# The gated recurrence's factor chain interleaved with the last eight projection blocks

## The chip, the cores and the metric

The kernel runs on one core of a Trainium2 chip. The metric is the device time of one execution in microseconds (us). It has five engines with their own instruction queues: TensorE (PE, with its weight loads shown as PEld), VectorE (DVE), ScalarE (ACT), GpSimd (POOL) and SyncE (SP, which here only issues DMAs). Each queue is worked off in order, and engines wait for each other through semaphores. All times on the axis "us" are counted from the start of the profiled span.

## What is computed

The reference is one transformer block followed by a second one. The part that matters here is the token mixing of the first block: the input of 512 tokens, normed, is multiplied with a wide matrix, and 16 blocks of 128 columns of the product feed a gated linear recurrence with 4 heads of 128. Its four inputs are q, f, i and og (4 blocks each).

```python
q = silu(q_raw); f = lb + (1 - lb) * sigmoid(f_raw); k = 1 - f; v = i_raw
b = cumsum(log(f))                        # within chunks of 64 tokens
ref = b at token 31 of the chunk; b_last = b at token 63
scores = (q * exp(b - ref)) @ (k * exp(ref - b)).T, causal, within a chunk
kv_n = (k * exp(b_last - b)).T @ v        # one state update for each chunk
state = exp(b_last) * state + kv_n        # over the 8 chunks
out = scores @ v + (q * exp(b)) @ state_before
y = rmsnorm(out) * sigmoid(og)
```

The "factor chain" is the elementwise part: sigmoid, the affine map to f and k, log, the running sum over 64 tokens, two shifted copies of it, four exponentials and four products. Beside it stand 24 "gate" blocks, further projections whose results are biased and stored to device memory for later; 8 of them lie in this stage.

## The kernel before

Everything is fp32. A projection block is 8 steps (one for each 128 rows of the weights) of three matmuls of 128x512 (lines 615 to 617: high weights by high operand, high weights by low operand, low weights by high operand), so 24 matmuls into one of the PSUM banks 0 to 3, taken in turn. The weights of a block are one "unit" of 128x1024: SP loads it (L453), ACT makes its high part (`split`, L1214, called by `units`), POOL its low part (`low`, L539). There are four slots for units, and ACT's `units(1)` beside block m splits the unit of block m+3, which it may do once PE has finished block m-1. `blocks(k)` on ACT is k such splits. Behind each unit's load SP also issues one 512 KB copy of a table that is needed much later (L462).

A bank is given back when DVE has copied it out (`copy_blocks`, L1890, semaphore `block_free`, counted in order); PE waits for that in `claim` before it writes the bank again. In the stage at hand (PE lines 888 to 941), blocks 0 to 3 are q (tile `hg_q`), 4 to 7 f (`hg_f`), 8 to 11 i (`hg_i`), 12 to 15 og (`hg_og`). Then PE turns the four heads of i (`turn`, L719: four 128x128 transposes of a head into bank 4 or 7, which ACT copies out by `turned`, L1334, before the bank is used again), runs six gate blocks (banks 0 and 1 in turn; ACT adds the bias and copies out, L1238, semaphore `gate_ready`, and issues the store, L1242), waits for `hg_factors_ready`, turns the four heads of K2, does the 32 score products (L911), and then alternates seven state products (L922) with quarters of the two remaining gate blocks.

ACT (lines 1540 to 1566) does all nine remaining splits first, then waits until all 16 blocks are copied out, then Silu of q, Sigmoid of f, Sigmoid of og, the four `turned` of V, the log, five gate copies (`gate1`), and when DVE has signalled `hg_shift`, the exponentials Q1, K1, Q2, DEC and, behind the second shift, K2; then the sixth gate copy and the four `turned` of K2. A change of function set costs ACT a table load, shown as ACT_TABLE_LOAD.

DVE (lines 2150 to 2183) copies out blocks 7 to 15 first and then runs its part of the chain: four affine maps (L2157), k (L2159), six scan steps of a copy and an addition each (L2166, L2167), two shifts (L2173), four products (L2179 to L2183). The second shift waits for two exponentials, because it overwrites their input.

Of the kernel before, what the change touches and what calls it, by code (L numbers as in the profile page):

```python
# [11 lines left out]
ACT = mybir.ActivationFunctionType  # L12
AX_X = mybir.AxisListType.X

P = 128
TOK = 512
TT = TOK // P
# [186 lines left out]
def program(nc, a):  # L204

    with ExitStack() as ctx:
# [380 lines left out]
        def _(pe):  # L587
# [45 lines left out]
            def x_ops():  # L633
                return (lambda k: XH[:, k, :]), (lambda k: XL[:, k, :])
# [4 lines left out]
            def operand(total):  # L639

                n["operand"] = n.get("operand", 0) + total
                pe.wait_ge(sem("operand_ready"), n["operand"])
# [249 lines left out]
            operand(DC)  # L892
            for m in range(8, 16):
                block_(DC, *x_ops())


            pe.wait_ge(sem("block_free"), n["freed"])
            for h in range(HEADS):
                turn([ZI[:, h, t * P:(t + 1) * P] for t in range(TT)])
# [298 lines left out]
        def _(act):  # L1198
# [341 lines left out]
            blocks(9)  # L1540

            act.wait_ge(sem("block_free"), n["freed"])
            act.activation(ZQ[:], ZQ[:], ACT.Silu).then_inc(sem("hg_q_ready"), 1)
            act.activation(ZF[:], ZF[:], ACT.Sigmoid).then_inc(sem("hg_sigmoid"), 1)
            act.activation(ZOG[:], ZOG[:], ACT.Sigmoid).then_inc(sem("hg_og_ready"), 1)
            for h in range(HEADS):
                turned(VT[:, h, :])
            act.dma_start(TRI[:], a["tri"]).then_inc(sem("tri_loaded"), 16)
            act.wait_ge(sem("hg_f_ready"), 1)
            act.activation(B0[:], ZF[:], ACT.Ln).then_inc(sem("hg_log"), 1)  # L1550
            for _ in range(5):
                gate1()
# [9 lines left out]
            gate1()  # L1562
            for h in range(HEADS):
                turned(K2T[:, h, :])
# [302 lines left out]
        def _(dve):  # L1867
# [284 lines left out]
            for z in (ZI, ZOG):  # L2152
                copy_blocks(z, 4)
            st.skip(8, 0)
# [4 lines left out]
            dve.tensor_scalar(KF[:], ZF[:], -1.0, 1.0, ALU.mult, ALU.add).then_inc(sem("hg_f_ready"), 1)  # L2159
            dve.wait_ge(sem("hg_log"), 1)  # L2160
# [3 lines left out]
            for i in range(6):  # L2164
                src, dst = chunks[i % 2], chunks[1 - i % 2]
                link(dve.tensor_copy(dst[:, :, 0:d], src[:, :, 0:d]))  # L2166
                link(dve.tensor_tensor(dst[:, :, d:CH], src[:, :, d:CH], src[:, :, 0:CH - d], ALU.add))  # L2167
                d *= 2

# [5 lines left out]
            shifted(CH // 2 - 1, 1)  # L2175
            dve.wait_ge(sem("hg_exp"), 2)
            shifted(CH - 1, -1)
            dve.wait_ge(sem("hg_q_ready"), 1)
# [689 lines left out]
```

## Time and profile before

| quantity | value |
|---|---|
| median of 3 runs | 3729.67 us |
| lowest, highest run | 3727.66, 3734.19 us |
| profiled execution: device time | 3727.16 us |
| profiled execution: span of the trace | 3725.3 us |
| busy share of the span: PE, PEld, DVE, ACT, POOL | 95%, 80%, 56%, 37%, 49% |
| mean granted TensorE clock | 0.976 of full speed |

The device time is 1.86 us longer than the span, which runs from the first to the last instruction. The profile's clock column is the share of TensorE's full clock (2.4 GHz) that was granted: 1.00 is 2.4 GHz and 0.50 is 1.2 GHz. The stage of the recurrence lies at 487 to 698 us of 3725. A share of PE's busy time over the whole span hides what happens in so short a stage, so the stage has to be read from its own waits and stretches. "x8" behind a row means that instructions of one kind that follow each other directly are merged, and the duration is that of all. The bracket at the end of a row of the timeline is the engine's idle time just before and who ended it.

### The profile page before, as it was taken

Reading aid. Unit: us, or ns where it says so; the run is one execution under the profiler, and the core shown is the slowest. Engines: PE = TensorE matmul, PEld = TensorE weight load, DVE = VectorE, ACT = ScalarE, POOL = GpSimd, SP = SyncE. Lnnn points to the kernel's source line nnn. Section 1 sums busy time; section 2 is a strip of 40 time slices with the busy share of each in tenths; the row PEclk is TensorE's granted clock in tenths of the full one; section 3 lists DMA queues with packets and bytes.
Section 4 is the critical chain, followed back from the end, with each engine's and each line's share of the span. In section 5 each row is a group of like instructions: output and inputs, shape, how many; then the busy total and the mean of one; then the engine's idle time right before and its main releaser. Section 6 shows DMA issues by size and latency. Waiting matters only on the chain. (4 is left out here: it accounts for less than half of the span.)

```text
span 3725.3 us, 49795 instructions
## 1 busy us (share of the span) xinstructions
PE 3532.4 (95%) x17547; PEld 2996.4 (80%) x17547; DVE 2092.5 (56%) x4197; ACT 1386.8 (37%) x1941; POOL 1838.5 (49%) x909
## 2 busy tenths in 40 slices
PE   8999997999999999997988999989999999999999
PEld 5777766777787688773676766779999999999999
DVE  4653055222234344125666255459999997677776
ACT  4333234233244322222323345323345454444443
POOL 5676433233243344341333301435566676788886
PEclk9999998999999999997999999999999999999999
DMA  6997544444567299331424312685559999899996
GB/s 241 386 381 247 159 150 140 127 149 149 158 206 246 72 297 290 113 100 42 137 80 134 101 54 71 220 325 176 164 164 317 344 352 342 325 388 391 383 383 234
DMA packets 458130, 813.81 MB, mean 218 GB/s; under 512 B 31544, under 2 KB 308984, under 8 KB 455322
## 3 DMA queue, kind: packets, MB, share of 16 engines
q1 hardware_dynamic: 278416, 436.07, 35.5%
q10 hardware_dynamic: 142666, 241.11, 18.3%
q0 software_dynamic: 36864, 134.23, 9.5%
q8 instruction: 108, 1.77, 0.2%
q14 instruction: 76, 0.62, 0.1%
HBM read 682.84 MB, written 195.56 MB: 236 GB/s over the span
## 5 line engine op out<-in xcount | busy, mean ns | idle before, releaser
L539 POOL TENSOR_TENSOR weights_lo<-weights_raw,weights_hi 128x1024 fp32r<-128x1024 f32 x649 | 1592.7, 2459 | 1816.1 <-ACT weights_hi L1214 1692.7
L615 PE MATMUL bank<-operand_hi,weights_hi 128*128 128x512 f32 (+1 forms) x2856 | 1093.4, 383 | 54.3 <-DVE operand_lo L1916 18.7
L617 PE MATMUL bank<-operand_hi,weights_lo 128*128 128x512 f32 (+1 forms) x2856 | 1064.5, 373 | 0.0
L616 PE MATMUL bank<-operand_lo,weights_hi 128*128 128x512 f32 (+1 forms) x2856 | 1063.4, 372 | 0.0
L1214 ACT ACTIVATE weights_hi<-weights_raw 128x1024 fp32r<-128x1024 f32 x649 | 683.3, 1056 | 858.6 <-PE bank L617 559.4
L615 PEld LDWEIGHTS bank<-operand_hi,weights_hi 128*128 128x128 f32 x2856 | 541.3, 190 | 145.9 <-DVE operand_lo L1916 25.1
L616 PEld LDWEIGHTS bank<-operand_lo,weights_hi 128*128 128x128 f32 x2856 | 542.1, 190 | 74.4 <-issue 5.5
L617 PEld LDWEIGHTS bank<-operand_hi,weights_lo 128*128 128x128 f32 x2856 | 540.2, 189 | 74.7
L615 PE MATMUL bank<-expert_hi,weights_hi 128*128 128x384 f32 x1024 | 345.1, 337 | 0.0
L617 PE MATMUL bank<-expert_hi,weights_lo 128*128 128x384 f32 x1024 | 345.0, 337 | 0.0
L616 PE MATMUL bank<-expert_lo,weights_hi 128*128 128x384 f32 x1024 | 345.0, 337 | 0.0
L615 PEld LDWEIGHTS bank<-expert_hi,weights_hi 128*128 128x128 f32 x1024 | 192.3, 188 | 0.0
L617 PEld LDWEIGHTS bank<-expert_hi,weights_lo 128*128 128x128 f32 x1024 | 192.3, 188 | 0.0
L616 PEld LDWEIGHTS bank<-expert_lo,weights_hi 128*128 128x128 f32 x1024 | 192.3, 188 | 0.0
L2632 DVE SCALAR_TENSOR_TENSOR bank<-gathered_experts,slot_weight,bank 128x512 f32<-128x512 f32 x254 | 178.8, 749 | 16.5 <-DMA gathered_experts<-expert_table_v,expert_index 14.6
L1773 ACT ACTIVATE gate_stage<-bank 128x512 f32<-128x512 f32 x96 | 104.2, 1086 | 175.3 <-PE bank L1133 162.5
L1960 DVE STREAM_TRANSPOSE expert_turned<-expert_rows 128x1024 f32<-128x1024 f32 x90 | 111.7, 1242 | 101.4 <-DMA expert_table_u<-expert_turned 79.8
L2541 DVE CUSTOM_DVE_ANT_0 gathered_experts<-gathered_experts,bank 128x512 f32<-128x512 f32 x256 | 161.9, 679 | 5.5 <-DMA gathered_experts<-expert_table_u,expert_index 5.4
L1821 ACT ACTIVATE expert_hi<-bank 128x384 fp32r<-128x384 f32 x128 | 63.0, 492 | 270.9 <-DVE bank L2580 264.7
L2557 DVE TENSOR_SCALAR one_hot_i<-iota,expert_ijg_t 128x128 f32<-128x128 f32 x384 | 160.1, 417 | 1.2 <-ACT expert_ijg_t L1334 1.2
L615 PE MATMUL bank<-hidden_hi,weights_hi 128*128 128x512 f32 x352 | 144.4, 410 | 2.0 <-DVE hidden_lo L2002 2.0
L617 PE MATMUL bank<-hidden_hi,weights_lo 128*128 128x512 f32 x352 | 139.5, 396 | 0.0
(397 smaller groups left out, 4899.5 us busy)
## 6 DMA issues: line engine op xcount, KB each, us to landing
weights_raw<-in_w_ffn_gu SPq DMA_DIRECT2D x132, 512.0 KB
expert_table_v<-in_w_peer_out SPq DMA_DIRECT2D x120, 512.0 KB, 5.5
weights_raw<-in_w_peer_ahead SPq DMA_DIRECT2D x120, 512.0 KB
weights_raw<-in_w_peer_out SPq DMA_DIRECT2D x120, 512.0 KB
expert_table_u<-expert_turned ACTq DMA_DIRECT2D x360, 128.0 KB, 4.7
expert_rows<-in_w_peer_ahead ACTq DMA_DIRECT2D x82, 512.0 KB, 6.7
peer_gates<-gate_stage SPq DMA_DIRECT2D x24, 1024.0 KB
expert_gates<-peer_gates ACTq DMA_DIRECT2D x16, 1536.0 KB
```

Of the source, the lines that this page charges most:

```text
L539: pool.tensor_tensor(LO[:, slot, :], RAW[:, slot, :], HI[:, slot, :].bitcast(F32), ALU.subtract).then_inc(sem("lo_ready"), 1)
L615: pe.matmul(out, wh, hi(k), start=(k == 0), stop=False)
L616: pe.matmul(out, wh, lo(k), start=False, stop=False)
L617: ins = pe.matmul(out, wl, hi(k), start=False, stop=(k == kc - 1))
L1214: act.activation(HI[:, slot, :], RAW[:, slot, :], ACT.Copy).then_inc(sem("hi_ready"), 1)
L1773: act.activation(STG[:, s, :, 4 * (q % 4):4 * (q % 4) + 4].rearrange("p j t -> p t j"), BANK[5 + q % 2][:].rearrange("p (t j) -> p t j", t ...
L1821: act.activation(dst, src, ACT.Copy).then_inc(sem("expert_high"), 1)
L1960: return dve.transpose(dst[:].rearrange("p (b c y) -> p c b y", b=4, c=DC), src[:].rearrange("p (c b y) -> p c b y", b=4, c=DC))
L2541: ins = dve.tensor_tensor_reduce(half, half, tokens_in[h][:], 1.0, 0.0, ALU.mult, ALU.add, DOT[:, s, h:h + 1])
L2557: dve.tensor_scalar(OI[:, u, :], IOTA[:], IJGT[:, 0, token], None, ALU.is_equal)
L2632: ins = dve.scalar_tensor_tensor(sums_of[h][:], half, AW[:, s:s + 1], sums_of[h][:], ALU.mult, ALU.add)
```

## The change

PE turns heads 0 and 1 of i behind block 13 and heads 2 and 3 behind block 14, having waited only for the copies of blocks 8 to 11, and no longer waits for all 16 blocks. ACT works the sigmoid of f, the log, the Silu of q and the copies of V in between its splits, does the exponentials right behind, and moves the sigmoid of og and five of the gate copies behind them. DVE starts its chain behind block 7 and puts the copies of blocks 8 to 15 in between the steps of the chain. No arithmetic is added or taken away; the products, the kv part and what follows are as they were.

```diff
--- before.py
+++ after.py
@@ -890,13 +890,15 @@
             for m in range(3, 8):
                 block_(DC, *rest)
             operand(DC)
+            inputs = n["freed"] + 4
             for m in range(8, 16):
                 block_(DC, *x_ops())
-
-
-            pe.wait_ge(sem("block_free"), n["freed"])
-            for h in range(HEADS):
-                turn([ZI[:, h, t * P:(t + 1) * P] for t in range(TT)])
+                if m == 13:
+                    pe.wait_ge(sem("block_free"), inputs)
+                for h in {13: (0, 1), 14: (2, 3)}.get(m, ()):
+                    turn([ZI[:, h, t * P:(t + 1) * P] for t in range(TT)])
+
+
             for _ in range(6):
                 gate_block()
             pe.wait_ge(sem("hg_factors_ready"), 1)
@@ -1537,19 +1539,22 @@
             highs(XH, XFM, 3, None, 3)
             blocks(1)
             highs(XH, XFM, 2, None, 6)
-            blocks(9)
-
-            act.wait_ge(sem("block_free"), n["freed"])
-            act.activation(ZQ[:], ZQ[:], ACT.Silu).then_inc(sem("hg_q_ready"), 1)
+            blocks(2)
+            act.wait_ge(sem("block_free"), n["freed"] - 1)
             act.activation(ZF[:], ZF[:], ACT.Sigmoid).then_inc(sem("hg_sigmoid"), 1)
-            act.activation(ZOG[:], ZOG[:], ACT.Sigmoid).then_inc(sem("hg_og_ready"), 1)
-            for h in range(HEADS):
-                turned(VT[:, h, :])
-            act.dma_start(TRI[:], a["tri"]).then_inc(sem("tri_loaded"), 16)
+            blocks(1)
             act.wait_ge(sem("hg_f_ready"), 1)
             act.activation(B0[:], ZF[:], ACT.Ln).then_inc(sem("hg_log"), 1)
-            for _ in range(5):
-                gate1()
+            blocks(1)
+            act.activation(ZQ[:], ZQ[:], ACT.Silu).then_inc(sem("hg_q_ready"), 1)
+            blocks(3)
+            for h in range(2):
+                turned(VT[:, h, :])
+            blocks(1)
+            for h in range(2, HEADS):
+                turned(VT[:, h, :])
+            blocks(1)
+            act.dma_start(TRI[:], a["tri"]).then_inc(sem("tri_loaded"), 16)
 
             act.wait_ge(sem("hg_shift"), 1)
             act.activation(Q1[:], B1[:], ACT.Exp).then_inc(sem("hg_exp"), 1)
@@ -1560,6 +1565,10 @@
             act.wait_ge(sem("hg_shift"), 2)
             act.activation(K2[:], B1[:], ACT.Exp).then_inc(sem("hg_exp"), 1)
             gate1()
+            act.wait_ge(sem("block_free"), n["freed"])
+            act.activation(ZOG[:], ZOG[:], ACT.Sigmoid).then_inc(sem("hg_og_ready"), 1)
+            for _ in range(5):
+                gate1()
             for h in range(HEADS):
                 turned(K2T[:, h, :])
             for _ in range(2):
@@ -2149,14 +2158,12 @@
 
             normed(XFM, HT, XH, XL, TOK, lambda c: vec("mix_pre", c), beside=first_blocks)
             copy_blocks(ZF, 3, first=1, scaled=True)
-            for z in (ZI, ZOG):
-                copy_blocks(z, 4)
-            st.skip(8, 0)
             dve.wait_ge(sem("hg_sigmoid"), 1)
             for h in range(HEADS):
                 link(dve.tensor_scalar(ZF[:, h, :], ZF[:, h, :], LB[:, 5, h:h + 1], LB[:, 2, h:h + 1],
                                        ALU.mult, ALU.add))
             dve.tensor_scalar(KF[:], ZF[:], -1.0, 1.0, ALU.mult, ALU.add).then_inc(sem("hg_f_ready"), 1)
+            copy_blocks(ZI, 1)
             dve.wait_ge(sem("hg_log"), 1)
 
             chunks = [b[:].rearrange("p h (n c) -> p (h n) c", c=CH) for b in (B0, B1)]
@@ -2166,6 +2173,10 @@
                 link(dve.tensor_copy(dst[:, :, 0:d], src[:, :, 0:d]))
                 link(dve.tensor_tensor(dst[:, :, d:CH], src[:, :, d:CH], src[:, :, 0:CH - d], ALU.add))
                 d *= 2
+                if i in (0, 1, 3):
+                    copy_blocks(ZI, 1, first=(1, 2, 2, 3)[i])
+                elif i >= 4:
+                    copy_blocks(ZOG, 1, first=i - 4)
 
             def shifted(at, sign):
                 edge = chunks[0][:, :, at:at + 1].to_broadcast([P, HEADS * NCH, CH])
@@ -2173,8 +2184,11 @@
                 dve.tensor_tensor(chunks[1], *pair, ALU.subtract).then_inc(sem("hg_shift"), 1)
 
             shifted(CH // 2 - 1, 1)
+            copy_blocks(ZOG, 1, first=2)
             dve.wait_ge(sem("hg_exp"), 2)
             shifted(CH - 1, -1)
+            copy_blocks(ZOG, 1, first=3)
+            st.skip(8, 0)
             dve.wait_ge(sem("hg_q_ready"), 1)
             link(dve.tensor_tensor(Q1[:], Q1[:], ZQ[:], ALU.mult))
             link(dve.tensor_tensor(K1[:], K1[:], KF[:], ALU.mult))
```

## Rows read from the trace of the kernel before

**Rows 1.** The page, busy time and share of each engine.

```profile
PE 3532.4 (95%) x17547; PEld 2996.4 (80%) x17547; DVE 2092.5 (56%) x4197; ACT 1386.8 (37%) x1941; POOL 1838.5 (49%) x909
```

**Rows 2.** Busy time by stretch of the stage; the first line names the columns.

```profile
core 0: us, PE busy (x) PEld busy (x) DVE busy (x) ACT busy (x) POOL busy (x), PEclk, DMA share, GB/s
530.90:574.40 43.50, 43.50 (x193) 35.84 (x191) 5.54 (x8) 9.78 (x9) 19.12 (x8) 1.00 0.63 193
574.40:618.70 44.30, 37.16 (x161) 30.46 (x160) 30.47 (x19) 25.17 (x23) 16.36 (x5) 0.92 0.56 172
618.70:639.60 20.90, 6.58 (x82) 5.80 (x81) 15.86 (x8) 9.47 (x11) 4.72 (x2) 0.59 0.21 68
```

**Rows 3.** The two longest PE waits, 570 to 680 us: total, times, longest.

```profile
PE bank L719 <- DVE hg_k L2183: 14.3, 1, 14.3
PE bank L719 <- ACT hg_v L1334: 6.4, 1, 6.4
```

**Rows 4.** PE's timeline: start, duration, line, tiles, idle before.

```profile
575.36 1.09 PE L719 MATMUL bank<-identity,hg_i 128*128 128x128 f32 x8 [0.79 <-DVE hg_og L1896]
582.81 1.97 PE L719 MATMUL bank<-identity,hg_i 128*128 128x128 f32 x8 [6.36 <-ACT hg_v L1334]
584.43 0.78 PE L615 MATMUL bank<-operand_hi,weights_hi 128*128 128x512 f32 x1
...
587.73 0.39 PE L617 MATMUL bank<-operand_hi,weights_lo 128*128 128x512 f32 x1
...
633.04 3.77 PE L719 MATMUL bank<-identity,hg_k 128*128 128x128 f32 x16 [14.32 <-DVE hg_k L2183]
636.74 2.92 PE L911 MATMUL bank<-hg_q,hg_k 128*64 128x64 f32 x64
```

**Rows 5.** The clock in one stretch of the second i turn.

```profile
582.20:584.90 2.70, 2.09 (x9) 2.09 (x10) 1.79 (x3) 1.72 (x5) 0.00 (x0) 0.50 0.03 6
```

**Rows 6.** DVE's timeline of the stage.

```profile
536.53 0.69 DVE L1896 COPY hg_i<-bank 128x512 f32<-128x512 f32 x1 [4.75 <-PE bank L617]
...
574.61 0.69 DVE L1896 COPY hg_og<-bank 128x512 f32<-128x512 f32 x1 [4.75 <-PE bank L617]
580.51 2.29 DVE L2157 TENSOR_SCALAR hg_f<-hg_f,lower_bound 128x512 f32<-128x512 f32 x4 [5.20 <-ACT hg_f L1544]
582.83 1.23 DVE L2159 TENSOR_SCALAR hg_k<-hg_f 128x2048 f32<-128x2048 f32 x1
...
588.91 2.26 DVE L2167 TENSOR_TENSOR hg_b<-hg_b 128x2016 f32<-128x2016 f32 x1
591.21 2.28 DVE L2166 COPY hg_b<-hg_b 128x64 f32<-128x64 f32 x1
...
602.73 2.02 DVE L2167 TENSOR_TENSOR hg_b<-hg_b 128x1792 f32<-128x1792 f32 x1
...
611.10 4.36 DVE L2173 TENSOR_TENSOR hg_b<-hg_b 128x2048 f32<-128x2048 f32 x1
...
630.69 2.29 DVE L2183 TENSOR_TENSOR hg_k<-hg_k,hg_k 128x2048 f32<-128x2048 f32 x1
```

**Rows 7.** POOL's timeline: a low part alone and one that met DVE.

```profile
537.82 2.39 POOL L539 TENSOR_TENSOR weights_lo<-weights_raw,weights_hi 128x1024 fp32r<-128x1024 f32 x1 [3.04 <-ACT weights_hi L1214]
...
589.75 3.67 POOL L539 TENSOR_TENSOR weights_lo<-weights_raw,weights_hi 128x1024 fp32r<-128x1024 f32 x1 [16.90 <-ACT weights_hi L1214]
```

**Rows 8.** ACT's timeline of the stage.

```profile
531.15 1.06 ACT L1214 ACTIVATE weights_hi<-weights_raw 128x1024 fp32r<-128x1024 f32 x1 [4.56 <-PE bank L617]
...
577.27 1.28 ACT L1544 ACT_TABLE_LOAD   x1
578.56 1.91 ACT L1544 ACTIVATE hg_f<-hg_f 128x2048 f32<-128x2048 f32 x1
...
582.18 1.07 ACT L1334 ACTIVATE hg_v<-bank 128x512 f32<-128x512 f32 x2
...
591.62 0.69 ACT L1238 ACTIVATE squares<-bank,vectors 128x512 f32<-128x512 f32 x1 [2.03 <-PE bank L617]
```

## Prediction

> **What bounds the kernel now.** The page comes first: PE is busy for 95% of the span, and beside its own weight loads (80%) no engine for more than 56% [rows 1], so only time in which PE stands still, or runs at a low clock, can be won. Whether there is any in the stage that changes is seen in its stretches [rows 2]. From 530.9 to 574.4 us, blocks 8 to 15, PE is busy for all of 43.5 us, and DVE for 5.5 and ACT for 9.8: both idle beside a full PE. From 574.4 to 618.7 PE lacks 7.1 us, and from 618.7 to 639.6 it works 6.6 of 20.9. Its waits name the causes [rows 3]: 14.3 us on the last product of the factor chain (L2183) and 6.4 us on the first copy of V (L1334), which ACT reaches only behind three activations of 128x2048; 0.79 us, the bracket of the first turn, go to the last copy of og [rows 4]. So the chain, not PE, sets when the K2 turns begin. The DMA share in these stretches is 0.63, 0.56 and 0.21 [rows 2], so transfers do not set the end of them.
>
> **What the change takes away.** First the waits: 14.32 + 6.36 + 0.79 = 21.5 us [rows 4], if each is covered (below).
>
> Then the clock. Behind both long waits PE ran at the lower level: in the second pair of i turns the granted clock was 0.50, which is 1.2 GHz [rows 5], after 6.4 us of standing; the stretch of the K2 turns has a mean of 0.59 [rows 2]. What that cost is read from rows at either level. The second pair of i turns took 1.97 us where the first took 1.09 [rows 4]: 0.9 us. In the first gate block, 584.43 to 587.73 are eight starts of matmuls in 3.30 us [rows 4]. At full clock a block of 24 takes 5.44 us (copies at 536.53 and 574.61 are seven blocks apart [rows 6]: 38.08 / 7), eight starts 1.8 us: 1.5 us. The K2 turns took from 633.04 to 636.74, 3.7 us [rows 4]. At full clock PE needs 4 x 0.45 (eight transposes that started within 0.9, from the 1.09 less the tail of the last), but two banks wait for ACT's copies of some 0.6 us each [rows 8] and for the last gate copy before them; I take 3.0: 0.7 us. The 64 small matmuls of the scores took 2.9 us [rows 4]. Full clock gives between 1.45 (half) and 2.9; I take 1.9, nearer to the half because the turns halved: 1.0 us. Sum of the clock: 4.1 us, bounds 2.4 (no gain on scores and K2 turns) to 5.3.
>
> **What it adds.** PE gets one wait at block 13, satisfied by then, and two more changes between blocks and turns. No row shows such a change without a wait; the bound from above is the 0.79 us that the first turn waited, from below 0; I take 0.2. The 16 i transposes are moved, not added. ACT gets a fifth table load, 1.28 us [rows 8], because the sigmoid of og now stands behind the exponentials; it lies beside gate blocks.
>
> **Is the work really covered?** I lay the changed queues out by durations of the rows. Block m ends at 536.5 + 5.44 (m - 8).
> - ACT: the split of block 8 ends at 532.2 [rows 8]; table load 1.28 and Sigmoid 1.9 give f at 535.4.
> - DVE: four maps 2.3, k 1.23 (a fixed-scalar form at the rate of the maps, 2048 elements in one instruction, so at most their 2.3; I take 1.2) give f at 539.0; block 8 is copied out by 539.7. ACT does the log by 541.0 behind the split of block 9 at 537.7.
> - DVE's scan. In the kernel before, steps 0 to 3 ended at 604.75 and all six at 611.1, with the first addition at 588.91 [rows 6], so some 16 and 22.3 us, and one low part of POOL for each 5.4 us already lay beside them. That is the rate it will meet again. With the copies of blocks between them, 0.73 each, block 11 is given back by 541.0 + 16 + 2.2 = 559.3 and the first shift ends at 541.0 + 22.3 + 3.7 + 2.3 = 569.3, at worst two more us as the 4.36 shows [rows 6].
> - PE wants block 11's copy at 563.7, behind block 13: 4.4 us to spare. Turns 0.9, block 14 until 570.1, turns 0.9, block 15 until 576.4.
> - ACT copies V of heads 2 and 3 by 571.8 (1.07 for two [rows 8]), splits until 572.9, issues one DMA 0.35, table load 1.3: 574.5. The shift is ready. Q1, K1, Q2 at 1.8 each and DEC end at 580.3. DVE shifts again from 578.2, ends 580.5. K2 by 582.4, split of the fourth gate block's unit by 583.4, copy of gate 0 (0.69 [rows 8]) by 584.1.
> - PE: gate 0 from 576.4, gate 1 until 587.3. Gate 2 wants the bank of gate 0: 3.2 us to spare. ACT then loads a table, 1.3, does the Sigmoid of og, 1.9, a split, 1.1, and copies gate 1 by 589.4; gate 3 wants it at 592.7: 3.3 us. From then on the ring is as before.
> - DVE behind its second shift: one copy 0.7, four products 9.2, and one collision with a low part of 2.1: factors at 592.9. PE ends the sixth gate block at 576.4 + 32.6 = 609.0. The wait of 14.3 is gone with 16 us to spare.
>
> SP's loads and table copies follow POOL's low parts, and their number is the same; the next loads are three units ahead of PE, 16 us, so an ACT or POOL that is some us late does not reach PE. If one of the covers goes, its excess comes back to PE one for one.
>
> The next thing after the K2 turns, 0.2 us of issue and the scores, is the state part, whose pace PE and DVE share as before. **Sum:** 21.5 + 4.1 - 0.2 = 25.4 us. The profiled execution took 3727.16 (span 3725.3 plus 1.86 around it): 3701.8. It lies 2.5 below the median 3729.67, so the median is forecast at 3704.3.
>
> One rule of the Trainium skill bears on the covers. A low part alone took 2.39 us, and one that met an addition of DVE 3.67; the scan copy of 128x64 that began at 591.21 ended at 593.49, when the low part that began at 589.75 ended (593.42) [rows 6, 7]. "SBUF — State Buffer", section "SBUF: two separate sides", calls the port pair of VectorE and GpSimd an exclusive lock, held for the whole instruction by whichever came first, for DVE instructions with two SBUF inputs or in a two-port mode. By this rule the rows agree; it is what rival 3 is made of.
>
> **Rivals.**
> 1. Late copies of the gate banks. ACT now does everything in one line from 564 to 590, with only 3.2 us to spare twice. If that line is 3 to 12 us later than laid out (a copy of V that waits for PE, a shift that meets low parts), PE stands up to 9 us before gate 2 and the clock may fall. For it: the smallest slack of all. Against it: its terms are rows. Gain 16 to 25, middle 20: 3709.
> 2. PE's gain is given back later, or the change does not do what it says. The stage from 3000 us on could be paced by something that doesn't move with PE. A rule that would give this: the same page, section "A bandwidth-pool intuition that's wrong", calls HBM almost always the bottleneck end to end. Here the DMA share was 0.21 to 0.63 in the stage [rows 2], and loads are issued behind POOL's and PE's progress, so they move with PE. No gain would mean 3730, half of it 3717.
> 3. Slower: DVE's steps and POOL's low parts exclude each other, and now PE waits for what lies between the steps. The place is the line of 18 instructions up to the first shift (4 maps, k, 12 of the scan, the shift), behind it ACT's exponentials and so the gate banks. By rows a collision costs DVE up to 2.07 (4.36 against 2.29 [rows 6]). The line has 5.2 us to spare at the shift and 3.2 at the gates, 8.4 together. PE loses all of the 25.4 when it is 34 us late, 1.9 us for each of the 18 beyond what the scan's rows hold already. At the full 2.4 of a low part each, 43 us, the time is 25.4 - (43 - 8.4) = 9 us slower, 3739. Against it: POOL does one low part for each block, five or six in this line, not eighteen. It decides only if each low part hits three instructions, which an exclusive lock alone can't do.
>
> **How the numbers follow.** Forecast 0.74 (3699 to 3709), rival 1 0.13 (3705 to 3716), rival 2 0.10, of which 0.03 halfway at 3717 and 0.07 within 4 us of 3730, rival 3 0.03. The bounds of the unknown costs are 25.4 - 2.3 and + 1.4; the runs before scatter from 2 below to 4.5 above their median. So 3698 to 3716 holds some 0.86, and a little more than asked for is left in since one piece of slack is thin. About 0.2%, 7.5 us, is what a measurement of this kernel can tell from no change. Faster by more: 0.74 + 0.13 + 0.03 = 0.90; within: 0.07; slower: 0.03.
>
> **What the profile after would show.** Right: PE's three waits on L719 are gone, PE is busy throughout from 530 to about 610, the granted clock stays 1.00 there, the K2 turns begin near 609 and the state products near 614 instead of 639.6, and DVE's last product lies some 16 us ahead of the K2 turns. Rival 1: a wait of PE L615 on ACT's copy L1238 at 587 or 593. Rival 2: the state products 25 us earlier, but the span not, with a longer wait later. Rival 3: PE waits on DVE's copies (L1896) at 564, or on ACT behind DVE, and DVE rows of 4 us. Wrong would be the whole sum if the waits moved to PE's claims of banks, or if the stage were 25 us shorter and another part longer.

## The result, and the profile after

| | before | changed |
|---|---|---|
| median of 4 runs, measured together | 3728.66 us | 3703.52 us |
| lowest, highest | 3726.43, 3734.19 | 3697.55, 3707.28 |
| ratio, 95% interval | | 0.993, 0.9913 to 0.9946 |
| span of the profiled execution | 3725.3 us | 3698.8 us |
| mean granted clock | 0.976 | 0.978 |

The changed kernel is 25.1 us faster by these medians, where 25.4 were forecast (3704.3, measured 3703.5); the interval of the ratio allows 20.1 to 32.4 us. Measured a second time, against 15 runs of the kernel before, it was 30.3 us faster (r0 below). The interval of that ratio allows 24.6 to 34.7 us, so the two agree.

The stage by stretches, after (columns as in the first line; the clock is the eighth value, before the DMA share):

```profile
core 0: us, PE busy (x) PEld busy (x) DVE busy (x) ACT busy (x) POOL busy (x), PEclk, DMA share, GB/s
530.10:576.40 46.30, 46.30 (x214) 38.46 (x213) 31.05 (x26) 24.62 (x21) 23.01 (x8) 1.00 0.60 186
576.40:608.10 31.70, 31.70 (x141) 26.21 (x140) 17.91 (x7) 16.85 (x17) 19.48 (x6) 1.00 0.75 233
608.10:613.20 5.10, 4.14 (x82) 3.59 (x80) 0.69 (x2) 3.81 (x6) 0.21 (x1) 1.00 0.92 270
```

Against [rows 2]: PE is busy in all of 46.3 and of 31.7 us, DVE now works 31.1 us and ACT 24.6 beside the last eight blocks instead of 5.5 and 9.8, and the granted clock is 1.00 throughout, where it had been 0.92 and 0.59 from the end of the blocks on. POOL is busy for 42.7 us in the three stretches, and was for 40.2 in those of [rows 2].

PE's waits from 530 to 680 us, after (total, times, longest):

```profile
PE bank L615 <- DVE dil_qkv L1905: 6.2, 1, 6.2
PE bank L719 <- ACT hg_k2t L1336: 1.0, 1, 1.0
```

All three waits of [rows 3, 4] are gone. The wait for K2's copy is the one that the prediction put inside its 3.0 us for the K2 turns; the one of 6.2 us lies behind the stage and was there before the change too.

PE's timeline, after (start, duration, line, tiles):

```profile
562.78 1.03 PE L719 MATMUL bank<-identity,hg_i 128*128 128x128 f32 x8
...
569.13 1.03 PE L719 MATMUL bank<-identity,hg_i 128*128 128x128 f32 x8
...
608.11 1.03 PE L719 MATMUL bank<-identity,hg_k 128*128 128x128 f32 x8
610.10 1.14 PE L719 MATMUL bank<-identity,hg_k 128*128 128x128 f32 x8 [0.95 <-ACT hg_k2t L1336]
611.18 2.08 PE L913 MATMUL bank<-hg_q,hg_k 128*64 128x64 f32 x64
613.19 1.04 PE L924 MATMUL bank<-hg_v,hg_k2t 64*128 64x128 f32 x7
```

The second pair of i turns takes 1.03 us and not 1.97, the K2 turns 3.07 (611.18 - 608.11) and not 3.70, the scores 2.01 (613.19 - 611.18) and not 2.85 [rows 4]. Since other parts of the trace move by some us from one profile to the next, the experiments are read by one length: from the first matmul of block 8 to the first state product (L922 before, L924 after). It was 639.59 - 530.89 = 108.70 us and is 613.19 - 530.14 = 83.05: **25.65 us less**. From the state product to the end of the span it was 3085.7 us and is 3085.6. The other 0.75 us of the span lie ahead of the stage. That the two rests agree to 0.1 us is chance: over the profiles of all kernels here in which nothing behind the stage is altered, this rest lies between 3079.8 (e9) and 3085.7 us (before). In none of them is it longer than in the kernel before, so nothing that the trace shows was given back later.

The length after is accounted for: 14 blocks of 5.44 (8 projection and 6 gate blocks) are 76.2, two pairs of i turns 0.91 each (569.13 - 562.78 less a block), K2 turns 3.07, scores 2.01: 83.1 us. There is no room for a cost of changing between blocks and turns.

DVE's timeline, after, at the steps that the prediction used:

```profile
534.72 2.29 DVE L2163 TENSOR_SCALAR hg_f<-hg_f,lower_bound 128x512 f32<-128x512 f32 x4 [3.69 <-ACT hg_f L1544]
...
543.55 1.69 DVE L2173 COPY hg_b<-hg_b 128x64 f32<-128x64 f32 x1
545.28 2.23 DVE L2174 TENSOR_TENSOR hg_b<-hg_b 128x1984 f32<-128x1984 f32 x1
...
555.04 0.69 DVE L1905 COPY hg_i<-bank 128x512 f32<-128x512 f32 x1
...
564.05 2.28 DVE L2184 TENSOR_TENSOR hg_b<-hg_b 128x2048 f32<-128x2048 f32 x1
...
576.86 2.29 DVE L2184 TENSOR_TENSOR hg_b<-hg_b 128x2048 f32<-128x2048 f32 x1 [6.84 <-ACT hg_k L1561]
...
584.31 4.38 DVE L2196 TENSOR_TENSOR hg_q<-hg_q,hg_q 128x2048 f32<-128x2048 f32 x1
588.73 4.38 DVE L2197 TENSOR_TENSOR hg_k<-hg_k,hg_k 128x2048 f32<-128x2048 f32 x1
```

And ACT's:

```profile
563.41 1.09 ACT L1336 ACTIVATE hg_v<-bank 128x512 f32<-128x512 f32 x2 [4.76 <-PE bank L719]
...
573.11 1.92 ACT L1560 ACTIVATE hg_q<-hg_b 128x2048 f32<-128x2048 f32 x1
...
581.96 0.67 ACT L1240 ACTIVATE squares<-bank,vectors 128x512 f32<-128x512 f32 x1
...
587.10 0.66 ACT L1240 ACTIVATE squares<-bank,vectors 128x512 f32<-128x512 f32 x1
```

Block 11 is copied out by 555.7, the first shift ends at 566.3, and ACT comes to it only at 573.1. The copy of gate 0 ends at 582.6; gate 2 begins at 586.35 (608.11 less four blocks): 3.7 us to spare. The copy of gate 1 ends at 587.8, gate 3 begins at 591.8: 4.0. The factors are ready at 593.1, 15.0 us ahead of the K2 turns.

### The profile page after: what moved, and what is told of

It reads as the page before. It is cut to its first block and busy times, and to the rows that moved or that the text cites. A ratio compares the mean times of both kernels' runs of the same rounds, so it can differ in the third digit from the quotient of the medians.

```text
span 3698.8 us, 49801 instructions
## 1 busy us (share of the span) xinstructions
PE 3528.6 (95%) x17547; PEld 2993.7 (81%) x17547; DVE 2091.1 (57%) x4197; ACT 1387.2 (38%) x1942; POOL 1842.2 (50%) x909
## 5 line engine op out<-in xcount | busy, mean ns | idle before, releaser
L615 PEld LDWEIGHTS bank<-operand_hi,weights_hi 128*128 128x128 f32 x2856 | 541.4, 190 | 145.2 <-DVE operand_lo L1925 24.6
L2646 DVE SCALAR_TENSOR_TENSOR bank<-gathered_experts,slot_weight,bank 128x512 f32<-128x512 f32 x254 | 178.8, 750 | 20.8 <-DMA gathered_experts<-expert_table_v,expert_index 18.9
L2572 DVE TENSOR_SCALAR one_hot_j<-iota,expert_ijg_t 128x128 f32<-128x128 f32 x384 | 142.7, 372 | 0.0
```

Of the source, the lines that this page charges most:

```text
L615: pe.matmul(out, wh, hi(k), start=(k == 0), stop=False)
L2572: return dve.tensor_scalar(OJ[:, u, :], IOTA[:], IJGT[:, 1, token], IJGT[:, 2, token], ALU.is_equal, ALU.mult)
L2646: ins = dve.scalar_tensor_tensor(sums_of[h][:], half, AW[:, s:s + 1], sums_of[h][:], ALU.mult, ALU.add)
```

## Experiments

Lengths are those from block 8 to the first state product; the changed kernel has 83.05. The last column has the device time and that of the kernel before measured with it; where a kernel ran once only, no conclusion is drawn from its time, as the profiles reach block 8 anywhere between 528.9 and 538.2 us and the rest behind the stage varies by 6 us.

| kernel | length, us | against changed | time; before, us (runs) |
|---|---|---|---|
| before | 108.70 | +25.65 | |
| changed; again (r0) | 83.05; 83.06 | | r0 3701.16; 3731.45 (5; 15) |
| e1 before, early i turns alone | 107.80 | +24.75 | 3726.32; 3731.45 (10; 15) |
| e2 changed, i turns late | 84.52 | +1.47 | 3705.97; 3728.24 (1; 1) |
| e10 changed, block copies behind the scan | 92.35 | +9.30 | 3709.69; 3728.24 (1; 1) |
| e3 changed, 2 more exponentials | 83.50 | +0.45 | 3703.13; 3731.31 (1; 1) |
| e4 changed, 5 more exponentials | 91.70 | +8.65 | 3709.31; 3731.31 (1; 1) |
| e5 changed, 4 more products | 86.07 | +3.02 | 3701.77; 3731.31 (1; 1) |
| e6 changed, 9 more products | 98.27 | +15.22 | 3721.92; 3731.31 (1; 1) |
| e9 before, PE kept busy | 106.70 | +23.65 | 3724.38; 3728.24 (1; 1) |
| e7 changed, sums before the dilated blocks | 83.06 | +0.01 | 3697.29; 3728.24 (1; 1) |
| e8 as e7, and K2 turns around gate 5 | 81.86 | -1.19 | 3693.99; 3731.45 (5; 15) |
| e11 as e8, split behind the norm's exponential | 81.86 | -1.19 | 3698.11; 3730.56 (4; 7) |

### Repeat, and where the time is

r0 is the changed kernel unaltered.

> The changed kernel unaltered, beside the kernel before and the next two on the same chip. My theory (the stage alone is shorter: 21.5 us of waits and about 4 us of low clock gone, all else moved forward as a whole): 25.6 us under the kernel before, ratio 0.9931; the first state product about 26 us earlier. Rival (part of the gain is given back in a later stage): the stage 25 us shorter but the time less than 20 us.

Measured: 3701.16 us against 3731.45, ratio 0.992 (0.9907 to 0.9934). The length is 83.06, and the rest behind it 3083.2 us, not longer than the 3085.7 of the kernel before. The stage alone is shorter, as the first theory has it.

### Which part of the change carries the gain

e1 takes only the turns:

```diff
             for m in range(8, 16):
                 block_(DC, *x_ops())
+                if m == 13:
+                    pe.wait_ge(sem("block_free"), inputs)
+                for h in {13: (0, 1), 14: (2, 3)}.get(m, ()):
+                    turn([ZI[:, h, t * P:(t + 1) * P] for t in range(TT)])
```

with ACT's four `turned` of V between its last splits. DVE's order is that of the kernel before.

> The kernel before with one part of the change: PE turns i behind blocks 13 and 14 and ACT copies V there; the factor chain stays where it was, behind block 15. Theory (one chain, from the last block copied out to the factors, sets when the K2 turns begin, so a wait of PE before it is worth nothing by itself): PE's waits of 0.8 and 6.4 us go, but its wait for the factors grows from 14.3 to about 20; the chain begins 1 us earlier because ACT has no V copies in front of the log; also a new wait of some 2.7 us before the third gate block. Gain 1 us. Rival (the waits add up, each is worth its length, as the prediction's sum has it): gain 0.8 + 6.4 + 2.4 of clock = 9.5 us.

e1's waits of PE in the stage:

```profile
PE bank L719 <- DVE hg_k L2189: 18.9, 1, 18.9
PE bank L615 <- ACT squares L1240: 2.2, 1, 2.2
```

The waits of 0.8 and 6.4 us are gone, and the wait for the factors has grown from 14.3 to 18.9. The length falls by 0.90 us, where lengths that add up would have given 9.5. The turns in front of it make the last block come 1.8 us later, and the chain from that block's copy to the factors takes 55.6 instead of 58.4 us, since V is copied by then. The runs went from 3731.45 to 3726.32 us (ratio 0.9985, 0.9975 to 0.9995), a gain of 1.9 to 9.3 us by the interval. That leaves out the 9.5 narrowly and the 0.9 too; the length in the trace is of one execution each, and where the runs' other microseconds come from stays open. A wait in front of another wait on the same chain was worth next to nothing: PE only arrives earlier at the later one.

e2 is the other half, the early chain without the early turns (PE still asks only for blocks 8 to 11 before it turns i):

```diff
-                if m == 13:
+                if m == 15:
                     pe.wait_ge(sem("block_free"), inputs)
-                for h in {13: (0, 1), 14: (2, 3)}.get(m, ()):
+                for h in {15: (0, 1, 2, 3)}.get(m, ()):
```

> The changed kernel with the four i turns back behind block 15 and ACT's copies of V behind its last split; the chain stays early. Theory: PE waits about 0.4 us for the two banks, and ACT's exponentials start 5 us later (578.3 instead of 573.1), which is more than the 3.7 us that the first gate copy had to spare, so PE waits 1.3 to 1.8 us before the third gate block: the first state product 2 us later than in the changed kernel. Rival (the early turns carry their full 7 us of waits and 2.4 of clock): 9 us later.

```profile
PE bank L719 <- ACT hg_k2t L1336: 1.0, 1, 1.0
PE bank L615 <- ACT squares L1240: 0.7, 1, 0.7
PE bank L719 <- ACT hg_v L1336: 0.3, 1, 0.3
```

These waits of PE (beside the 6.2 behind the stage) are 0.7 us before the third gate block and 0.3 between the turns. The length grows by 1.47 us, where 2 were expected. So 24.2 of the 25.65 us come with the early chain alone, 0.9 with the early turns alone. The early turns are worth little in either order, 0.9 us without the early chain and 1.5 with it; the early chain is worth nearly everything in either. It also takes away the waits at the turns of i: with the turns in their old place only 0.3 us of the old 7.2 is left there, since ACT no longer has Silu and two Sigmoids to do in front of V.

### Why the copies stand between the scan steps

e10:

```diff
-                if i in (0, 1, 3):
-                    copy_blocks(ZI, 1, first=(1, 2, 2, 3)[i])
-                elif i >= 4:
-                    copy_blocks(ZOG, 1, first=i - 4)
+                if i == 5:
+                    copy_blocks(ZI, 3, first=1)
+                    copy_blocks(ZOG, 2)
```

> The changed kernel with DVE's copies of blocks 9 to 13 behind all six scan steps and not between them. Theory: the scan ends near 560.5, block 13 cannot have the bank of block 9 before 561.2 and not at 557.3 as in the changed kernel: PE waits 3.8 us there, and the first state product comes 3.8 us later, with no further wait (the clock stays full, ACT moves with PE). Rival (the copies beside the scan cost DVE's chain more than they save PE): no wait of PE on a copy, and the first state product no later.

DVE's timeline of e10, and the block of PE that waited:

```profile
541.57 0.35 DVE L2173 COPY hg_b<-hg_b 128x32 f32<-128x32 f32 x1 [1.39 <-ACT hg_b L1547]
...
544.24 2.30 DVE L2173 COPY hg_b<-hg_b 128x64 f32<-128x64 f32 x1
...
560.81 3.25 DVE L2174 TENSOR_TENSOR hg_b<-hg_b 128x1024 f32<-128x1024 f32 x1
564.09 1.89 DVE L1905 COPY hg_i<-bank 128x512 f32<-128x512 f32 x3
```

```profile
564.93 0.76 PE L615 MATMUL bank<-operand_hi,weights_hi 128*128 128x512 f32 x1 [6.13 <-DVE hg_i L1905]
```

The mechanism is as expected, the size is not: 9.3 us against 3.8. The scan was expected to end at 560.5 us on the changed kernel's axis, and ended at 562.8 on it (564.1 less 1.3, by which e10's block 8 starts later), so the wait was 2.3 us longer than expected. It took 22.5 us (541.57 to 564.06) without any copy in between; in the changed kernel it took 23.2 (540.26 to 563.41) with four copies of 0.69 in between. The four copies, 2.8 us by themselves, cost 0.7. POOL's rows of the changed kernel show why:

```profile
542.50 2.68 POOL L539 TENSOR_TENSOR weights_lo<-weights_raw,weights_hi 128x1024 fp32r<-128x1024 f32 x1 [1.94 <-ACT weights_hi L1216]
547.95 2.40 POOL L539 TENSOR_TENSOR weights_lo<-weights_raw,weights_hi 128x1024 fp32r<-128x1024 f32 x1 [2.77 <-ACT weights_hi L1216]
553.38 3.89 POOL L539 TENSOR_TENSOR weights_lo<-weights_raw,weights_hi 128x1024 fp32r<-128x1024 f32 x1 [3.04 <-ACT weights_hi L1216]
```

The copy of block 11 (555.04 to 555.73) ran while POOL's low part of 553.38 to 557.27 was under way, and took its 0.69 us. It reads PSUM. The additions and copies of the scan have their inputs in SBUF and do not run beside a low part: the copy of 128x64 at 543.55 takes 1.69 us and ends at 545.24, 0.06 us after the low part of 542.50. Put between them, the PSUM copies used time in which the chain would have stood anyway. Behind the wait of 6.1 us the clock was at 0.50 until 571 us, which is the other 3.2 of the 9.3.

### How late ACT may be

e3 and e4 put two and five more exponentials in front of the first one:

```diff
             act.wait_ge(sem("hg_shift"), 1)
+            for i in range(5):
+                act.activation(Q1[:], B1[:], ACT.Exp).then_inc(sem("padded"), 1)
+                act.wait_ge(sem("padded"), i + 1)
             act.activation(Q1[:], B1[:], ACT.Exp).then_inc(sem("hg_exp"), 1)
```

> The changed kernel with two more exponentials of 128x2048 on ACT before the first one, 3.8 us with their waits: it makes the line of ACT late on purpose. Theory (the gate banks have 3.7 us to spare, more comes back one for one): PE waits 0 to 0.5 us before the third gate block, the first state product at most 0.5 us later. Rival (the slack is not real, a later ACT is felt at once): 3.8 us later.

> The changed kernel with five more exponentials on ACT before the first one, 9.5 us. Theory: PE waits 5.8 us before the third gate block and nowhere else in the stage, and the clock may fall for a few us behind it; the first state product 5.8 to 7 us later. Rival (the ring of two banks passes the lateness on to the next gate blocks): 9 us or more.

In e3 PE waited 0.15 us, and the length is 0.45 us greater; the other 0.3 us stay unexplained. e4, PE's row at the third gate block, and the clock of four stretches around it (eighth value):

```profile
593.49 0.77 PE L615 MATMUL bank<-operand_hi,weights_hi 128*128 128x512 f32 x1 [5.99 <-ACT squares L1240]
```

```profile
589.00:591.00 2.00, 0.00 (x0) 0.00 (x0) 2.00 (x3) 1.59 (x3) 0.00 (x0) 1.00 0.00 0
591.00:593.00 2.00, 0.00 (x0) 0.00 (x0) 1.97 (x2) 2.00 (x3) 0.07 (x1) 0.69 0.01 4
593.50:598.00 4.50, 4.50 (x11) 3.57 (x12) 4.47 (x2) 4.24 (x4) 3.75 (x1) 0.50 0.16 58
599.00:602.00 3.00, 3.00 (x15) 2.47 (x14) 2.96 (x2) 1.33 (x2) 3.00 (x2) 1.00 0.96 311
```

The spare time is real: 3.8 us of lateness cost 0.45, and of 9.5 us PE waited 6.0. Beyond it the price is more than one for one. The wait is the one expected (5.8), the price is above the expected 5.8 to 7: the clock fell while PE stood and stayed at 1.2 GHz for some 5 us behind the wait, 8.65 - 5.99 = 2.7 us more. The wait occurred once, so the ring did not pass it on, and the rival falls.

### How late DVE may be

e5 and e6 put four and nine more products of 128x2048 in front of DVE's first:

```diff
+            for _ in range(4):
+                link(dve.tensor_tensor(SC[:].rearrange("p h t c -> p (h t c)"),
+                                       ZQ[:].rearrange("p h t -> p (h t)"),
+                                       KF[:].rearrange("p h t -> p (h t)"), ALU.mult))
             link(dve.tensor_tensor(Q1[:], Q1[:], ZQ[:], ALU.mult))
```

> The changed kernel with four more products of 128x2048 on DVE before its first product, at least 9.2 us; with their collisions with POOL's low parts up to 17. Theory (factors have 15.0 us to spare, from 593.1 to PE's K2 turns at 608.1): the factors at 602.4 to 608, no wait of PE for them, the first state product within 0.5 us of the changed kernel's. Rival (the lock starves POOL and PE waits for a low part of the weights): a wait of PE on L539 and 2 us or more.

> The changed kernel with nine more products on DVE, at least 20.7 us. Theory: factors at 614 to 620, so PE waits 6 to 12 us for them, the granted clock falls in that wait if it is long enough (it fell in the kernel before within waits of 6.4 and 14.3 us), and the K2 turns and scores take 1 to 1.6 us more: the first state product 6 to 14 us later. Rival (POOL's low parts come late as well): a wait of PE on L539 before the factors are late.

DVE's products in e5, then PE's K2 turns in e5 and in e6:

```profile
583.16 13.43 DVE L2194 TENSOR_TENSOR hg_scores<-hg_q,hg_k 128x2048 f32<-128x2048 f32 x4
596.63 4.38 DVE L2195 TENSOR_TENSOR hg_q<-hg_q,hg_q 128x2048 f32<-128x2048 f32 x1
...
609.85 4.36 DVE L2199 TENSOR_TENSOR hg_k<-hg_k,hg_k 128x2048 f32<-128x2048 f32 x1
```

```profile
614.26 3.49 PE L719 MATMUL bank<-identity,hg_k 128*128 128x128 f32 x16 [2.50 <-DVE hg_k L2199]
```

```profile
630.47 3.77 PE L719 MATMUL bank<-identity,hg_k 128*128 128x128 f32 x16 [14.16 <-DVE hg_k L2199]
```

Eight products took from 583.2 to 614.2, 31.0 us instead of 8 x 2.3 = 18.4. POOL did six low parts in that time, so each cost DVE 2.1 us. The factors of e5, expected at 602 to 608 on the changed kernel's axis, came at 610.7 there (614.2 less 3.5, by which its block 8 starts later), and PE waited 2.5 us. There was no wait of PE on a low part, so the rival falls: what comes late is DVE. The theory of e5 fails too, since it had no wait at all and at most 0.5 us. The clock had fallen within those 2.5 us; e5's clock just before the turns and in their first 3 us (eighth value):

```profile
613.00:614.00 1.00, 0.00 (x0) 0.00 (x0) 1.00 (x1) 0.00 (x0) 0.00 (x0) 0.96 0.88 147
614.00:617.00 3.00, 2.73 (x13) 2.36 (x14) 1.97 (x2) 1.20 (x2) 0.00 (x0) 0.50 1.00 332
```

Eight of the turns took 1.97 us, as at the lower level in [rows 4]. In e6 the wait is 14.2 us, above the 6 to 12 expected, and the turns take the 3.77 us that they took in the kernel before; the length grows by 15.2, above the 14 of the range. In e5 the 9.2 us of added work made DVE 17.6 us late at the factors (610.7 against 593.1). By that ratio the 15.0 us of spare time hold some 8 us of such work; this is an estimate, no run has that much.

### The clock by itself

e9 is the kernel before with matmuls of no use while PE would stand (they write a bank that is not in use):

```diff
             for h in range(HEADS):
                 turn([ZI[:, h, t * P:(t + 1) * P] for t in range(TT)])
+                if h == 1:
+                    idle_work(26)
             for _ in range(6):
                 gate_block()
+            idle_work(58)
             pe.wait_ge(sem("hg_factors_ready"), 1)
```

> The kernel before with 26 matmuls of no use between the second and third i turn and 58 before its wait for the factors, so that PE never stands still for long there; the wait itself stays with the chain. It tells the clock's share from the wait's. Theory (the clock costs what the rows at the two levels say): the granted clock stays 1.00 through the stage, K2 turns near 3.0 us instead of 3.7 and scores 2.0 instead of 2.9, the first gate block 5.4 and not 6.9; from the factors' end (633.0 in the kernel before) to the first state product 5.1 us instead of 6.6, so about 1.6 us gained, and up to 1 more if V is copied sooner. Rival (the clock's 4.1 us come back whatever the wait does): 4 us gained.

```profile
637.37 3.51 PE L719 MATMUL bank<-identity,hg_k 128*128 128x128 f32 x16 [2.36 <-DVE hg_k L2190]
```

The length falls by 2.0 us, where 1.6 to 2.6 were expected. DVE's chain was 0.9 us shorter (from its last block copy to the factors 57.5 instead of 58.4 us), since V was copied sooner; the rest, 1.1, is from the factors to the first state product, 5.5 us instead of 6.6. It is less than the 1.5 expected, because the useless work ended 2.4 us too soon and the granted clock was 0.50 again from 637.4 to 640 us, in most of the turns. So the clock behind the last wait of the chain cost about what the rows say. The first gate block ran at full clock now, and of the 2.0 us none is left for it: the clock behind an earlier wait cost nothing, because the later wait absorbed it. The rival (4 us whatever the wait does) falls. When PE's waits went in the changed kernel, though, no later wait was left to absorb anything, and there all of it counted.

### A version that is faster than both

The largest wait left near the stage is the 6.2 us on the first dilated block. e7 moves the sums of each head's norm by one block, e8 also turns heads 0 and 1 of K2 ahead of the sixth gate block:

```diff
                 for m in range(9):
-                    block_(DC, *x_ops())
                     if h == 0 and m < HEADS:
                         sums(1, ONES, TOK)
+                    block_(DC, *x_ops())
```

```diff
-            for _ in range(6):
+            for _ in range(5):
                 gate_block()
             pe.wait_ge(sem("hg_factors_ready"), 1)
-            for h in range(HEADS):
+            for h in range(2):
+                turn([K2[:, h, t * P:(t + 1) * P] for t in range(TT)])
+            gate_block()
+            for h in range(2, HEADS):
                 turn([K2[:, h, t * P:(t + 1) * P] for t in range(TT)])
```

> The changed kernel with only the sums for the norm of head h moved before dilated block h. Theory: PE's wait of 6.2 us on the copy of the first dilated block becomes about 0.8: the end 5.4 us earlier than in the changed kernel. Rival: the wait stays near 6, or a wait of PE for the squares of the same size takes its place.

> The changed kernel, with two PE orders altered: the sums for the norm of head h stand before dilated block h and not behind it, and the K2 turns of heads 0 and 1 stand before the sixth gate block, ACT's copies with them. Theory (PE's idle time in the trace is what can be won, wait by wait): the wait of 6.2 us on the copy of the first dilated block shrinks to about 0.8, and the 0.95 us between the K2 turns goes: 6.3 us under the changed kernel, 32 under the kernel before. Rival (the wait of 6.2 is set by DVE's own work there, not by when the sums come): 1 us under the changed kernel.

PE's only wait on that line in e8:

```profile
PE bank L615 <- DVE dil_qkv L1911: 1.9, 1, 1.9
```

It is 1.9 us in e7 and e8 and not 0.8. The missing 1.1 us is a collision that the new order brought about. DVE's product for the norm of the last head takes 1.84 us in e8 beside a low part, and 0.75 in the changed kernel, where none lies beside it:

```profile
663.17 1.84 DVE L2239 SCALAR_TENSOR_TENSOR hg_out<-hg_out,vectors,reciprocal_root 128x512 f32<-128x512 f32 x1 [3.78 <-ACT reciprocal_root L1295]
```

```profile
662.06 2.40 POOL L539 TENSOR_TENSOR weights_lo<-weights_raw,weights_hi 128x1024 fp32r<-128x1024 f32 x1 [3.95 <-ACT weights_hi L1219]
```

From the first state product to the block that waits it is 57.3 us instead of 61.5, which with the 1.2 of the K2 turns makes 5.4 us, where 6.3 were expected. By the runs e8 has 3693.99 us, 7.2 below the changed kernel measured with it; against the kernel before 0.9905 (0.9891 to 0.9918). This interval and that of the changed kernel overlap, so it is the trace that shows the 5.4 us, not the runs.

e11 tried for the rest by moving ACT's split behind the norm's logarithm and exponential:

```diff
                 square(OF[:, h, :], TOK, "hg_out_read", h + 1)
 
-                units(1)
                 root(TOK, P, read=("piece_made", n["f"] + h) if h else None, table=h == 0)
+                units(1)
```

> The kernel with sums before the dilated blocks and K2 turns around the sixth gate block, and ACT's split moved behind the logarithm and exponential of each head's norm. In the one without that, PE still waited 1.9 us where 0.8 was expected, and ACT's split (1.06 us), which now has to wait for PE's block, stood in front of the logarithm. Theory (that split is the rest): the wait falls from 1.9 to 0.9 us or less. Rival (DVE's own work at the end, four low parts and four copies, sets it): it stays at 1.9. The time about 1 us lower, too little for the runs to show; against the kernel before about 32 us.

The length of the stage is e8's, 81.86 us, but the wait grew to 5.1 us. DVE's rows and POOL's in e11:

```profile
662.09 0.75 DVE L2239 SCALAR_TENSOR_TENSOR hg_out<-hg_out,vectors,reciprocal_root 128x512 f32<-128x512 f32 x1 [4.87 <-ACT reciprocal_root L1295]
...
663.56 6.80 DVE L1929 TENSOR_TENSOR branch_lo<-hg_out,branch_hi 128x512 fp32r<-128x512 f32 x4
```

```profile
663.17 2.66 POOL L539 TENSOR_TENSOR weights_lo<-weights_raw,weights_hi 128x1024 fp32r<-128x1024 f32 x1 [3.71 <-ACT weights_hi L1219]
667.47 2.34 POOL L539 TENSOR_TENSOR weights_lo<-weights_raw,weights_hi 128x1024 fp32r<-128x1024 f32 x1 [1.64 <-ACT weights_hi L1219]
```

Counted from the first state product, DVE's product for the last head's norm starts only 0.1 us earlier than in e8, so the split in front of the logarithm had cost next to nothing. It ends 1.2 us earlier, because it no longer meets a low part (0.75 us, in e8 1.84). But the split moved behind now ends 2.1 us later, and its low part with it, so POOL's two low parts of 663.17 and 667.47 meet DVE's four low parts of the branch, which took 6.80 us instead of 2.49. What held PE up was not the split but where its low part falls. So the theory of e11 fails, and so does its rival, a wait that stays at 1.9. The time is 3698.11 us, ratio 0.9911 (0.9894 to 0.9928), which the runs can't tell from e8's; by the traces e8 is the best, as e11's way from the first state product to the waiting block is 3.1 us longer.

## Why the prediction was right, and where its steps were not

**The waits, 21.5 us.** All gone, and the sum came out. But the step that listed them as three separate gains was no account of their cause: e1 and e2 show that the early chain carries 24.2 of 25.65 us, and that of the 7.2 us of the first two waits, with their low clock, only 0.9 us could be won without it, and all but 1.5 us with it alone. The sum was right because the prediction had shown every wait covered at once. Had the chain stayed where it was, the same adding up would have said 9.5 us for 0.9.

**The clock, 4.1 us.** Second i turns 0.94 (0.9 taken), first gate block 1.5 (1.5), K2 turns 0.63 (0.7), scores 0.84 (1.0): 3.9 us. The scores took 2.01 us where 1.9 was assumed between bounds of 1.45 and 2.9. The upper bound of the clock's sum, 5.3, doesn't follow from its terms: with the scores and the K2 turns both halved they give some 5.7. The 3.9 us measured lie within either.

**What it adds, 0.2 us.** It adds nothing that the trace shows; the 83.05 us are used up without it.

**Sum.** 21.5 + 3.9 = 25.4 against 25.65; the remaining 0.25 us is assigned to nothing. That the median came out within 0.8 us of the forecast is in part luck, as the interval of the measurement is 12 us wide; the length of the stage is the better test of the sum. The fifth table load of ACT lay beside a gate block, as foreseen.

**The covers.** All held, most with more room. Block 11 was given back 7.0 us ahead of its use (4.4 forecast), the shift was ready at 566.3 and not 569.3, and ACT's line ran 0.7 us ahead of plan (the profile's stage starts 0.75 earlier; 582.6 against 584.1), so the gates had 3.7 and 4.0 us to spare and not 3.2 and 3.3. The scan was laid out as the old scan's length plus the copies; the copies cost hardly anything there. The factors came when they were due, at 593.1 against 592.9, but by errors against each other: two products met a low part, not one (2.1 us more), the second shift ended at 579.2 and not 580.5, and the prediction's own terms add up to 592.5.

**Rival 1** did not occur, and e4 shows it was real: 9.5 us of lateness would have cost 8.65. It named the fall of the clock, but its price, at most 9.4 us for a wait of up to 9, left nothing for it; in e4 a wait of 6.0 us cost 8.65.

**Rival 2** fell: behind the stage the kernel takes no longer than before. The transfers were at a share of 0.60 and 0.75 in the two long stretches, and PE's list of waits there has none but the two shown, so transfers did not set the time here. What the Trainium skill's "SBUF — State Buffer", section "A bandwidth-pool intuition that's wrong", says of HBM as the usual bottleneck did not apply to this stage.

**Rival 3** was priced with the right mechanism. In e5 six low parts in 31.0 us cost DVE 2.1 us each, close to the 2.07 taken; two of them lay in the four added products, which took 13.4 us instead of 9.2. The rule of the Trainium skill that the prediction named ("SBUF — State Buffer", section "SBUF: two separate sides"), a second comer blocked for the whole instruction, agrees with e5 and e11. The prediction's bound on it, one low part for each block and so five or six in the line up to the first shift, held too (six), and PE did not wait on that line, as it had concluded. Beside the products, where ACT's splits stand close behind each other, the bound doesn't hold: there four low parts lie in the 15.5 us from 582.2 to 597.7.

## What to carry to other kernels

Before adding up the waits of an engine, ask whether they lie on one chain: two waits ahead of a longer one, and the low clock behind them, were worth 0.9 us of 9.5 here as long as the longer one stood. Spare time of an engine that feeds TensorE should be counted to the microsecond, since what goes beyond it can cost more than its length through the clock: 3.0 us for a wait of 2.5 (e5), 8.65 for one of 6.0 (e4). Where VectorE's chain shares its time with GpSimd, try its PSUM copies between the chain's steps, which paid here, and look where the GpSimd instructions fall after each reordering.

## What the runs showed of the hardware

- VectorE instructions with their inputs in SBUF and GpSimd's 128x1024 subtractions did not overlap: each low part cost a run of products 2.1 us (12.6 over six in e5), while a 0.69 us copy from PSUM ran beside one at full speed (changed kernel, 555.04). In e1, four low parts followed each other directly (12.75 us from 590.32), and additions of 2.2 us took 4.3.
- When both wanted to go on, they alternated: in e5 each of the last four products took 4.36 to 4.38 us, a low part and its own 2.3.
- A low part moved 2.1 us later (e11) met four subtractions of VectorE, which so ran into the next low part as well and took 6.80 us instead of 2.49.
- Behind a wait of 2.5 us (e5) and one of 2.4 us (e9) the granted clock was 0.50; behind waits of 0.7 us (e2) and 1.9 us (e8) it stayed at 1.00. In e4 and e10, waits of 6.0 and 6.1 us cost 2.7 and 3.2 us more, with the clock at 0.50 behind them. These are single cases.
